# Sample attention moved from the last block's mixer into the first block's feed-forward part, the first gates of a block in two other PSUM banks, and constants set up before the row transposes

## The chip, the cores and the metric

The kernel runs on one core of one Trainium2 chip. The metric is device time in microseconds (us) of one execution. PE is the matrix engine (TensorE), PEld its weight loads, DVE the vector engine, ACT the scalar engine, POOL GpSimd, SP the engine that issues the weight transfers. PSUM has eight banks of 128 x 512 floats.

## What is computed

One layer of a hybrid decoder, for 2048 prompt rows and for 32 sample rows (8 sequences of 4 new tokens, each with a cache of 128 keys and values). Cut to what matters here:

```python
z = rmsnorm(x) @ w_in + b_in
q, k, v, xb, yb = split(z)
attn = sink_attend(q, band(k), band(v))          # prompt: window 128, in blocks of 128 queries
attn = sink_attend(q, [cache_k|k], [cache_v|v])  # sample rows: 128 cached and the new keys
xc = causal_conv(xb, prefix)
r, i = sigmoid(xc @ w_a + b_a), sigmoid(xc @ w_i + b_i)      # block-diagonal gates
lru = scan(exp(-8 r softplus(-lam)), sqrt(1 - a*a) * i * xc) # RG-LRU, in order of time
h = x + concat[attn, lru * gelu(yb)] @ w_out + b_out
y = h + (silu(gate) * up) @ w_ffn_out            # gate, up = rmsnorm(h) @ w_ffn_in
y = rmsnorm(y) * g_final
```

## The kernel before

All activations lie transposed (features on partitions). The prompt is worked through in four blocks of 512 rows; block 3, the last, is handled as "wide", that is with the 32 sample rows beside its 512, in two halves of 272 columns. The head (key, value and query projections) of block 0 is wide too and projects the 32 sample rows; their queries, keys and values lie in columns 512 to 543 from then on. Weights are split into a high and a low part, and each product is three matmuls (lines 657 to 659: high x high, high x low, low x high). The eight products of a weight tile ("unit") have 24 such matmuls per column range. Results go to three PSUM banks in rotation, `G[0..2]`; `S[0..1]`, `TB[0..1]` and `V` are the other five.

Each engine has its own queue, in an order that is written out by hand; semaphores tie them. A block is `head`, `mixers`, `ffn`. In `mixers` eight steps s = 0..7 follow on PE: `scores(s)` (L758, into S), `attend(s-2)` (L794, into V), on odd steps `spread` (L808), the unit of step s, on odd steps in its middle `gates(c)` with c = s // 2 (L817), and `probs_T(s-1)` (L776, into TB). `gates(c)` writes both S banks, so it waits for `xc_ready` (the convolution of tile c, DVE L1527 to L1529) and for `sc_read` (DVE has reduced the scores of this step, `softmax_1`, which ends in the small L1498). `scores` of an even step waits for `gates_read`, that is until ACT has read the gates (`lru_gates`, L1170 and L1171). ACT's exponentials of step s (`exps`, L1157) stand in its queue ahead of `lru_gates`, and DVE's `softmax_1(1)` stands behind `conv(0)`, whose input ACT writes (L1077) behind `exps(0)`.

The sample rows' attention and recurrence are steps within the mixer of block 3: `sample_load` (L889 ff., after step 1, transposes the cache), `sample_scores` (L906, step 4), `sample_probs` (L917, step 5), `sample_attend` (L929) and `sample_gates` (L940, both step 6), each with its part on DVE (L1650 ff., the convolution of the sample rows `sample_conv` L1709 to L1713) and ACT. Their scores, transposes and results use the S, TB and V banks too, so the prompt's steps wait for them. The cache comes in by seven transfers on POOL's queue, into the space of `hT`, at the start of block 3. POOL also loads the next block's rows, `load_x(b + 1)`, when a block's attention is done.

At the very start ACT copies the sample rows (L1336) and sums the squares of the rows (`x_stat`); DVE copies the transposed rows. The constants of the recurrence (about twenty operations on 128x4 elements that depend on each other, L1818 to L1837, one of them an exponential on ACT, L1347) are worked out after the head of block 0.

Of the kernel before, what the change touches and what calls it, by code (L numbers as in the profile page):

```python
# [31 lines left out]
ACT = mybir.ActivationFunctionType  # L32
# [59 lines left out]
def hymba_layer(nc, x_p, x_s, cache_k, cache_v, conv_in, h_in, units, vecs, w_a, w_i, sinks_p, sinks_s,  # L92
# [53 lines left out]
    with ctx:  # L146
# [38 lines left out]
        dist = place("dist", [P, 2 * WINDOW])  # L185
        dist_b = place("dist_b", [P, 2 * WINDOW])
        sinks = place("sinks", [P, NH])
# [33 lines left out]

        r = top[0]
        x_tok = place("x_tok", [P, QB, DM])
# [34 lines left out]

        SC = WINDOW + NS
        c_at = [h_at[0]]  # L260
        kc_tok = place("kc_tok", [P, DB, P], at=h_at)
        v_at = [h_at[0]]
        vc_tok = place("vc_tok", [P, DB, P], at=h_at)
        s_at = [h_at[0]]
        st_s = place("st_s", [(CONV_W - 1) * DB + DB, LC * P], at=h_at)
        k_at = [h_at[0]]
        kc_T = place("kc_T", [P, DB, P], at=h_at)
        dist_s = place("dist_s", [P, SC], at=h_at)
        s_s = place("s_s", [P, NKV, SC], at=h_at)
        q_r = place("q_r", [P, P], at=h_at)  # L270
        xc_s = place("xc_s", [P, LC, NS], at=h_at)
        hs0 = place("hs0", [P, LC, DB], at=h_at)
        assert h_at[0] <= h_end
        q_d = place("q_d", [P, DB, P], at=c_at)
        vs_tok = place("vs_tok", [NS, P], at=s_at)
        ks_out = place("ks_out", [NS, P], at=s_at)
        k_out = place("k_out", [P, P], at=s_at)
        mx_s = place("mx_s", [P, 6, NKV], at=s_at)
        pcT = place("pcT", [P, NKV, P], at=k_at)
        pnT = place("pnT", [NS, NKV, P], at=k_at)  # L280
        mixs = place("mixs", [P, KT, NS], at=k_at)
        l_s = [place(f"l_s{i}", [P, LC, NS], at=v_at) for i in range(6)]
        outc = place("outc", [P, LC, SCOLS], at=v_at)
# [253 lines left out]
        def _(pool):  # L537
# [27 lines left out]
            for b in range(NB - 1):  # L565

                amix_ready.wait(pool, b, QB)
                xT_done.wait(pool, b, KT)
                load_x(b + 1)
            b = NB - 1  # L570

            yT_done.wait(pool, b, 0)
            for dst, src in ((kc_tok[:, :, :], cache_k[0].rearrange("b s g d -> s b (g d)")),
                             (vc_tok[:, :, :], cache_v[0].rearrange("b s g d -> s b (g d)")),
                             (dist_s[:, :], dist_s_in)):
# [1397 lines left out]
```

## Time and profile before

| | |
|---|---|
| median of 3 runs | 2319.34 us (2317.89 to 2319.46) |
| the profiled execution | 2317.46 us, its span 2315.5 us |
| PE busy | 2235.7 us, 97% |
| DVE, ACT, POOL busy | 1163.2, 827.3, 32.2 us (50%, 36%, 1%) |
| mean granted clock of PE | 0.985 |

The profile's page gives busy time per engine; the trace behind it gives each instruction's start, the idle time of its engine just before it, and what ended that. In rows of the timeline merged instructions show their number as x8 and so on; one float32 matmul leaves two records. The granted clock 1.00 is 2.4 GHz and 0.50 is 1.2 GHz.

### The profile page before, as it was taken

How to read it: one execution, taken by the hardware profiler on the slowest of the kernel's cores; microseconds unless marked ns; L12 is line 12 of the kernel's file. 1: busy time of each engine (PE TensorE's matmuls, PEld its weight loads, DVE VectorE, ACT ScalarE, POOL GpSimd, SP SyncE). 2: the span in 40 equal slices, each digit the busy share in tenths (PEclk: the TensorE clock that was granted, in tenths of full speed). 3: DMA queues.
4: the chain of work that ended last, by engine and by line, in shares of the span. 5: the costliest groups of instructions: out<-in, count | busy, mean ns of one | idle time of the engine just before them, and what ended most of it. 6: DMA issues, size and time to landing. Idle time of an engine off the chain costs nothing.

```text
span 2315.5 us, 29680 instructions
## 1 busy us (share of the span) xinstructions
PE 2235.7 (97%) x12183; PEld 1886.6 (81%) x12183; DVE 1163.2 (50%) x2020; ACT 827.3 (36%) x1326; POOL 32.2 (1%) x66
## 2 busy tenths in 40 slices
PE   6999999999999999999999999999989799999997
PEld 6767888888777888888877888888878699999997
DVE  4586535446375544445466553544537545444444
ACT  4574222243274322234256322224326432222221
POOL 1000000000000000000000000000010000000000
PEclk8999999999999999999999999999999799999999
DMA  6445322222624222222533323232352132222221
GB/s 232 163 168 207 100 98 91 95 88 88 221 110 164 91 92 99 91 91 87 178 143 142 116 94 98 88 104 80 139 187 76 51 120 85 91 83 84 91 86 63
DMA packets 79014, 264.80 MB, mean 114 GB/s; under 512 B 9613, under 2 KB 13917, under 8 KB 78864
## 3 DMA queue, kind: packets, MB, share of 16 engines
q1 hardware_dynamic: 72288, 242.25, 30.4%
q0 software_dynamic: 3936, 12.03, 1.5%
q10 hardware_dynamic: 2656, 8.62, 0.9%
q8 instruction: 97, 1.59, 0.3%
q14 instruction: 37, 0.30, 0.0%
HBM read 231.04 MB, written 32.84 MB: 114 GB/s over the span
## 4 chain that ended last, share of the span: by engine, by line
PE 89%; DVE 5%; ACT 3%; issue 1%; DMA 1%; ACTq 0%; DVEq 0%
PE bank L657 27%; PE bank L659 27%; PE bank L658 27%; PE bank L817 1%; PE bank L794 1%; PE bank L758 1%; DMA out_y_p<-y_tok 1%; PE bank L776 1%; DVE s_p L1492 1%; DVE xc L1529 1%; PE bank L717 1%; PE bank L808 0%; PE bank L695 0%; PE bank L679 0%; DMA xs_tok<-in_x_sample 0%
## 5 line engine op out<-in xcount | busy, mean ns | idle before, releaser
L657 PE MATMUL bank<-x_hi,w_hi 128*128 128x512 f32 (+1 forms) x2208 | 786.6, 356 | 7.3 <-DVE x_lo L1424 4.8
L659 PE MATMUL bank<-x_hi,w_lo 128*128 128x512 f32 (+1 forms) x2208 | 777.9, 352 | 0.0
L658 PE MATMUL bank<-x_lo,w_hi 128*128 128x512 f32 (+1 forms) x2208 | 776.8, 352 | 0.0
L1052 ACT ACTIVATE w_hi<-w_raw 128x1024 fp32r<-128x1024 f32 (+1 forms) x294 | 304.6, 1037 | 1022.2 <-PE bank L659 992.5
L657 PEld LDWEIGHTS bank<-x_hi,w_hi 128*128 128x128 f32 x2208 | 416.5, 189 | 78.3 <-issue 16.2
L658 PEld LDWEIGHTS bank<-x_lo,w_hi 128*128 128x128 f32 x2208 | 416.8, 189 | 59.0 <-issue 2.9
L659 PEld LDWEIGHTS bank<-x_hi,w_lo 128*128 128x128 f32 x2208 | 416.1, 188 | 57.3
L657 PE MATMUL bank<-a_hi,w_hi 128*128 128x512 f32 (+1 forms) x1168 | 413.7, 354 | 10.3 <-DVE a_lo L1575 3.9
L1383 DVE TENSOR_TENSOR w_lo<-w_raw,w_hi 128x1024 fp32r<-128x1024 f32 (+1 forms) x294 | 351.2, 1195 | 142.5 <-ACT w_hi L1052 142.2
L659 PE MATMUL bank<-a_hi,w_lo 128*128 128x512 f32 (+1 forms) x1168 | 413.0, 354 | 0.0
L658 PE MATMUL bank<-a_lo,w_hi 128*128 128x512 f32 (+1 forms) x1168 | 412.4, 353 | 0.0
L657 PEld LDWEIGHTS bank<-a_hi,w_hi 128*128 128x128 f32 x1168 | 221.0, 189 | 45.6 <-issue 7.9
L658 PEld LDWEIGHTS bank<-a_lo,w_hi 128*128 128x128 f32 x1168 | 221.0, 189 | 30.8
L659 PEld LDWEIGHTS bank<-a_hi,w_lo 128*128 128x128 f32 x1168 | 220.9, 189 | 30.7
L1790 DVE TENSOR_TENSOR hT<-bank,hT 128x512 f32<-128x512 f32 (+1 forms) x120 | 71.0, 591 | 232.2 <-PE bank L659 232.2
L1397 DVE TENSOR_TENSOR gt<-bank,rinv 128x512 f32<-128x512 f32 (+1 forms) x110 | 64.9, 591 | 227.3 <-PE bank L659 203.0
L1397 DVE TENSOR_TENSOR a<-bank,rinv 128x512 f32<-128x512 f32 (+1 forms) x110 | 65.1, 592 | 215.9 <-PE bank L659 213.9
L1157 ACT ACTIVATE s_p<-s_p,nm 128x256 f32<-128x256 f32 x128 | 63.4, 497 | 36.1 <-DVE sd L1498 36.1
L1320 ACT ACTIVATE a_hi<-a 128x512 fp32r<-128x512 f32 (+1 forms) x88 | 56.3, 640 | 35.8 <-DVE a L1780 33.8
L1776 DVE SCALAR_TENSOR_TENSOR gt<-th,gt 128x512 f32<-128x512 f32 (+1 forms) x88 | 61.1, 695 | 6.0 <-ACT th L1317 5.9
L1780 DVE SCALAR_TENSOR_TENSOR a<-gt,a 128x512 f32<-128x512 f32 (+1 forms) x88 | 61.6, 700 | 3.0
L1784 DVE TENSOR_TENSOR a_lo<-a,a_hi 128x512 fp32r<-128x512 f32 (+1 forms) x88 | 61.0, 693 | 0.0
(282 smaller groups left out, 1627.5 us busy)
## 6 DMA issues: line engine op xcount, KB each, us to landing
w_raw<-in_units SPq DMA_DIRECT2D x222, 512.0 KB, 3.2
w_raw<-in_units SPq DMA_DIRECT2D x64, 448.0 KB, 3.1
w_hi<-keep SPq DMA_DIRECT2D x51, 512.0 KB, 3.2
w_lo<-keep SPq DMA_DIRECT2D x51, 512.0 KB, 4.2
w_kept<-keep SPq DMA_DIRECT2D x30, 512.0 KB, 4.4
keep<-w_hi SPq DMA_DIRECT2D x22, 512.0 KB, 4.9
keep<-w_lo SPq DMA_DIRECT2D x22, 512.0 KB, 5.5
x_tok<-in_x_prompt POOLq DMA_DIRECT2D x16, 512.0 KB, 5.9
```

Source lines behind the costliest of these rows:

```text
L657: nc.tensor.matmul(out, h, hi[:, kt, c0:c1], start=(first and kt == kts[0]), stop=False)
L658: nc.tensor.matmul(out, h, lo[:, kt, c0:c1], start=False, stop=False)
L659: mm = nc.tensor.matmul(out, l, hi[:, kt, c0:c1], start=False, stop=(kt == kt_of[u] - 1))
L1052: A(w_hi[:, slot(b, u), 0:n], w_raw[:, u % RAW, 0:n], ACT.Copy).then_inc(w_hi_ready, 1)
L1157: A(s_p[:, s % 2, hh, :], s_p[:, s % 2, hh, :], ACT.Exp, bias=nm[:, s % 2, hh:hh + 1], accum_out=rs[:, s % 2, hh:hh + 1])
L1320: act_hi.by(A(a_hi[:, f, 0:w], a32[:, n % 2, 0:w], ACT.Copy))
L1383: TT(w_lo[:, slot(b, u), 0:n], w_raw[:, u % RAW, 0:n], w_hi[:, slot(b, u), 0:n], ALU.subtract).then_inc(w_ready, 1)
L1397: return lambda src, c0, c1: TT(dst(c0, c1), src, rinv[:, c0:c1], ALU.mult)
L1776: link(STT(out=gt[:, 0:w], in0=th[:, 0:w], scalar=1.0, in1=gt[:, 0:w], op0=ALU.add, op1=ALU.mult))
L1780: act_f.by(STT(out=a32[:, n % 2, 0:w], in0=gt[:, 0:w], scalar=0.5, in1=a32[:, n % 2, 0:w], op0=ALU.mult, op1=ALU.mult))
L1784: act_ready.by(TT(a_lo[:, f, 0:w], a32[:, n % 2, 0:w], a_hi[:, f, 0:w], ALU.subtract))
L1790: evacuate(b, last, u, lambda src, c0, c1: TT(hT[:, m, c0:c1], src, hT[:, m, c0:c1], ALU.add))
```

## The change

1. `sample_load`, `sample_q`, `sample_scores`, `sample_max`, `sample_exps`, `sample_norm`, `sample_probs` and `sample_attend` run in block 0's feed-forward part, behind the pairs of units f = 1 to 5 of its first chunk. Their tiles lie in the space of `x_tok` (the next block's rows), the result `mixs` in the space of `dist_b`. POOL issues the seven cache transfers when block 0's attention is done, and loads the rows of block 1 only when the sample attention is finished and the new keys and values are written out. `sample_gates`, `sample_conv` and the recurrence of the sample rows stay in block 3.
2. In `sample_scores` and `sample_attend` the two key-value heads (two halves of the array's rows, or now of its columns) alternate, where one followed the other.
3. The first gates of a block (c = 0) go into `V` and a free `G` bank, and wait no more for `sc_read`. In blocks 0 to 2 they stand one product earlier within their unit.
4. The constants are set up before the row copies; ACT waits for them before its first copy.
5. The transpose of the prompt's last keys moves to the head of block 3. `dist_b` is used in block 0 alone, and its copy at the end of each block's mixer goes.

```diff
@@ gates and their banks
+        def gate_banks(c, wide):
+            return S if c else (V, G[1 if wide else 2])
...
                 def gates(c):
                     xc_ready.wait(pe, b, c + 1)
-                    sc_read.wait(pe, b, 2 * c + 2)
+                    if c:
+                        sc_read.wait(pe, b, 2 * c + 2)
                     for n in range(2):
-                        mm = nc.tensor.matmul(S[n][:, :], gates_w[:, n, c, :], xc[:, c % 2, :],
+                        mm = nc.tensor.matmul(gate_banks(c, last)[n][:, :], gates_w[:, n, c, :], xc[:, c % 2, :],
                                               start=True, stop=True)
...
-                        gemm(b, last, UH + s, x_hi, x_lo, None, list(range(KT - 2)))
+                        cut = KT - 3 if s == 1 else KT - 2
+                        gemm(b, last, UH + s, x_hi, x_lo, None, list(range(cut)))
...
-                        for step in sample_at.get(s, ()):
-                            step(b, s)
+                        if s == 6:
+                            sample_gates(s)
@@ PE, sample attention
-            def sample_load(b, s):
+            def sample_load():
+                rinvh_ready.wait(pe, 0, 1)
+                gates_read.wait(pe, 0, LC)
                 pe.wait_ge(smp_in, 16 * 7)
-                pTa_ready.wait(pe, b, s)
-                pTb_ready.wait(pe, b, s)
...
+                for bb in range(DB):
+                    for g in range(NKV):
+                        r = slice(g * HEAD, (g + 1) * HEAD)
+                        nc.tensor.matmul(S[g][:, 0:WINDOW], q_d[r, bb, :], kc_T[r, bb, :],
+                                         start=(bb == 0), stop=(bb == DB - 1))
...
-            sample_at = {1: (sample_load,), 4: (sample_scores,), 5: (sample_probs,), 6: (sample_attend, sample_gates)}
+            sample_at = {1: sample_load, 2: sample_scores, 4: sample_probs, 5: sample_attend}
...
+                        if b == 0 and ci == 0 and f in sample_at:
+                            sample_at[f]()
@@ ACT
                         act_hi.by(A(a_hi[:, f, 0:w], a32[:, n % 2, 0:w], ACT.Copy))
+                        if b == 0 and n == 2:
+                            sample_exps()
...
             split(0, 0)
+            act.wait_ge(first_in, 16 * N_FIRST)
+            act.wait_ge(setup_done, 2)
+            A(set_t[:, 1, :], set_t[:, 0, :], ACT.Exp, scale=-1.0).then_inc(setup_act, 1)
+            act.wait_ge(setup_done, 3)
             act.wait_ge(smp_pe, 1)
-            act.wait_ge(first_in, 16 * N_FIRST)
             chain.link(A(xT[:, :, T:W], V[:, 0:KT * NS].rearrange("p (k n) -> p k n", k=KT), ACT.Copy))
@@ DVE
-                        d = dist_b if qb == 0 else dist
+                        d = dist_b if b == 0 and qb == 0 else dist
...
-            sample_at = {1: sample_load, 4: sample_max, 5: sample_probs, 6: sample_attend}
-            sample_after = {2: sample_q, 7: sample_gelu}
+            sample_at = {1: (sample_load, sample_q), 2: (sample_max,), 3: (sample_norm,), 4: (sample_probs,),
+                         5: (sample_attend,)}
@@ POOL
                 amix_ready.wait(pool, b, QB)
                 xT_done.wait(pool, b, KT)
+                if b == 0:
+                    for dst, src in ((kc_tok[:, :, :], cache_k[0].rearrange("b s g d -> s b (g d)")),
...
+                    pool.wait_ge(smp_dve, SMP_DVE_L)
...
+                    pool.wait_ge(smp_dve, SMP_DVE_AT)
+                    pool.wait_ge(kv_out, 16 * 2 * DT)
                 load_x(b + 1)
```

PE at the first gates of block 0 (unit of step 1), before; `x_hi`, `x_lo` with `w_hi`, `w_lo` are the unit's products, three rows each:

```order
L657 MATMUL bank<-x_hi,w_hi 128x512
L658 MATMUL bank<-x_lo,w_hi 128x512
L659 MATMUL bank<-x_hi,w_lo 128x512
L817 MATMUL bank<-xc,gates_w 128x512 [waits sc_read,xc_ready]
L817 MATMUL bank<-xc,gates_w 128x512
L657 MATMUL bank<-x_hi,w_hi 128x512 [waits w_ready]
```

And in the changed kernel, up to the scores of step 2 (L771):

```order
L672 MATMUL bank<-x_hi,w_lo 128x512
L825 MATMUL bank<-xc,gates_w 128x512 [waits xc_ready]
L825 MATMUL bank<-xc,gates_w 128x512
L670 MATMUL bank<-x_hi,w_hi 128x512 [waits w_ready]
...
L672 MATMUL bank<-x_hi,w_lo 128x512
L787 MATMUL bank<-ident,s_p 128x128 [waits v_ready,p_ready]
L787 MATMUL bank<-ident,s_p 128x128 x7
L771 MATMUL bank<-kT,qT 128x256 [waits gates_read]
L771 MATMUL bank<-kT,qT 128x256 x3
```

The gates wait for `xc_ready` alone, and three products instead of two follow them; the scores of step 2 still wait for `gates_read`.

PE in block 3 between steps 4 and 5, before, with the sample scores (L906, L908) between the transposes of step 3 and the scores of step 5:

```order
L776 MATMUL bank<-ident,s_p 128x128 [waits pTb_ready,pTa_ready,p_ready]
L776 MATMUL bank<-ident,s_p 128x128 x7
L906 MATMUL bank<-kc_T,q_d 128x128 [waits sc_read,smp_dve]
L906 MATMUL bank<-kc_T,q_d 128x128 x7
L908 MATMUL bank<-kT,q_r 128x32
L906 MATMUL bank<-kc_T,q_d 128x128 x8
L908 MATMUL bank<-kT,q_r 128x32
L758 MATMUL bank<-kT,qT 128x256 [waits smp_dve,sc_read]
```

The same work in the changed kernel, in block 0's feed-forward part between the units of f = 2 and f = 3:

```order
L671 MATMUL bank<-x_lo,w_hi 128x512
L672 MATMUL bank<-x_hi,w_lo 128x512
L913 MATMUL bank<-kc_T,q_d 128x128 [waits smp_dve]
L913 MATMUL bank<-kc_T,q_d 128x128 x15
L917 MATMUL bank<-kT,q_r 128x32 x2
L670 MATMUL bank<-x_hi,w_hi 128x512 [waits freed,w_ready]
```

It stands between units and nothing of the attention of the prompt waits for it. `sample_load`, `sample_probs` and `sample_attend` stand likewise behind f = 1, 4 and 5.

ACT in the changed kernel, from its first weight split (L1061) to the first exponentials of block 0 (L1166):

```order
L1061 ACTIVATE w_hi<-w_raw 128x1024 [waits raw_in0]
L1346 ACTIVATE set_t<-set_t 128x4 [waits setup_done,first_in]
L1349 ACTIVATE xT<-bank 128x8x32 [waits smp_pe,setup_done]
L1100 ACTIVATE y_tok,sum_x<-x_tok 128x1024 [waits x_in,zeroed,act_chain]
...
L1061 ACTIVATE w_hi<-w_raw 128x1024 [waits kept_out2,gemm_done,raw_in0]
L88 ISA
L1166 ACT_TABLE_LOAD [waits sc_read,y_out1]
L1166 ACTIVATE s_p,rs<-s_p,nm 128x256 [waits y_out0]
```

Before, the function table for the exponentials was loaded ahead of the constants' exponential, which stood behind that last weight split; now the load stands behind the wait for `sc_read`.

## Rows read from the trace of the kernel before

**Rows 1.** Window: length, busy PE, PEld, DVE, ACT, POOL, clock, DMA share, GB/s
```profile
220.00:560.00 340.00, 340.00 (x1492) 275.52 (x1491) 159.85 (x197) 104.41 (x131) 0.00 (x0) 1.00 0.28 93
```
**Rows 2.** Timeline of block 3's mixer, PE and DVE: start, duration, [idle before <- releaser]
```profile
1722.26 3.40 PE L817 MATMUL bank<-xc,gates_w 128*128 128x512 f32 x4 [4.72 <-DVE sd L1498]
...
1730.47 1.06 PE L889 MATMUL bank<-ident,kc_tok 128*128 128x128 f32 x8 [0.93 <-DVE pT L1512]
...
1734.54 1.08 PE L794 MATMUL bank<-pT,v_tok 128*64 128x256 f32 x8 [1.25 <-DVE kc_T L1656]
...
1764.56 2.16 PE L906 MATMUL bank<-kc_T,q_d 64*128 64x128 f32 x18
...
1769.83 2.09 PE L758 MATMUL bank<-kT,qT 64*128 64x256 f32 x8 [1.40 <-DVE mx_s L1678]
...
1784.08 0.30 PE L917 MATMUL bank<-ident,s_s 128*128 128x128 f32 x1 [0.93 <-DVE pT L1512]
...
1784.64 1.14 PE L758 MATMUL bank<-kT,qT 64*128 64x256 f32 x8
...
1794.77 2.29 DVE L1713 SCALAR_TENSOR_TENSOR xc_s<-xs_b,vec,xc_s 128x32 f32<-128x32 f32 x12
...
1797.93 1.86 PE L929 MATMUL bank<-pcT,vc_tok 128*64 128x16 f32 x16 [4.04 <-DVE pT L1512]
...
1802.77 3.62 PE L940 MATMUL bank<-xc_s,gates_w 128*128 128x32 f32 x16
...
1808.11 2.08 PE L758 MATMUL bank<-kT,qT 64*128 64x256 f32 x8 [1.72 <-ACT l_s L1273]
```
**Rows 3.** Timeline, first steps of block 1's mixer, PE and ACT
```profile
637.27 1.96 PE L817 MATMUL bank<-xc,gates_w 128*128 128x512 f32 x4 [1.78 <-DVE sd L1498]
...
639.98 0.69 ACT L1171 ACTIVATE ii<-bank,lru_c 128x512 f32<-128x512 f32 x1
...
641.41 1.14 PE L758 MATMUL bank<-kT,qT 64*128 64x256 f32 x8
```
**Rows 4.** Timeline of PE in block 2, and the window of the clock behind it
```profile
1178.24 2.96 PE L817 MATMUL bank<-xc,gates_w 128*128 128x512 f32 x4 [2.60 <-DVE sd L1498]
...
1184.03 1.14 PE L758 MATMUL bank<-kT,qT 64*128 64x256 f32 x8
...
1179.00:1180.00 1.00, 1.00 (x2) 0.34 (x1) 0.00 (x0) 1.00 (x5) 0.00 (x0) 0.52 0.00 0
```
**Rows 5.** Timeline of PE, DVE and ACT at the first steps of block 0
```profile
73.24 1.28 ACT L1347 ACT_TABLE_LOAD   x1
...
74.99 0.16 DVE L1818 TENSOR_SCALAR set_t<-vec 128x4 f32<-128x4 f32 x1
...
79.16 0.16 DVE L1837 TENSOR_SCALAR lru_c<-vec 128x4 f32<-128x4 f32 x1
...
81.55 1.14 PE L758 MATMUL bank<-kT,qT 64*128 64x256 f32 x8 [2.26 <-DVE sd L1498]
...
89.89 3.46 PE L817 MATMUL bank<-xc,gates_w 128*128 128x512 f32 x4 [2.84 <-DVE sd L1498]
...
95.71 1.14 PE L758 MATMUL bank<-kT,qT 64*128 64x256 f32 x8
```
**Rows 6.** Start of the kernel: ACT's timeline, and the transfer of `vec` (us to landing last)
```profile
3.02 0.51 ACTq L1040 DMA_DIRECT2D vec<-in_vecs  x1
...
13.98 0.38 ACT L1336 ACTIVATE xT<-bank 128x256 f32<-128x256 f32 x1 [6.30 <-PE bank L994]
...
vec<-in_vecs ACTq DMA_DIRECT2D x1, 37.0 KB, 7.2
```
**Rows 7.** Timeline of PE, block 3: matmuls on alternating halves of the columns
```profile
1744.64 1.04 PE L808 MATMUL bank<-ident,rec 128*64 128x128 f32 x16
```
**Rows 8.** POOL's timeline in block 0, and the cache's transfer (us to landing last)
```profile
171.50 2.13 POOL L540 DMA_DIRECT2D x_tok<-in_x_prompt  x4 [158.94 <-DVE a_lo L1575]
...
kc_tok<-in_cache_k POOLq DMA_DIRECT2D x1, 512.0 KB, 6.9
```

More of the change, by code:

```diff
@@ L569, in _ @@
                 load_x(b + 1)
             b = NB - 1
[L572 to L575, printed above, removed]
-                pool.dma_start(dst, src).then_inc(smp_in, 16)
-            for t in range(CONV_W - 1):
-                pool.dma_start(st_s[t * DB:(t + 1) * DB, :], conv_in[0, :, t, :]).then_inc(smp_in, 16)
@@ L835, in mixers @@
                     else:
-                        gemm(b, last, UH + s, x_hi, x_lo, None, [KT - 2, KT - 1])
+                        gemm(b, last, UH + s, x_hi, x_lo, None, list(range(cut, KT)))
                     if s >= 1:
@@ L1236, in mixers @@
                         lru_hi((s - 3) // 2)
-                    if last and s == 4:
-                        sample_exps()
                     if last and s == 6:
@@ L1591, in mixers @@
                         softmax_2(s - 1)
-                    if last and s == 5:
-                        sample_norm()
                     if last and s == 6:
@@ L1604, in mixers @@
                         probs_T(s - 1)
-                    if last and s in sample_at:
-                        sample_at[s]()
                     if s >= 3 and s % 2 == 1:
@@ L1610, in mixers @@
                         gelu_arg(c)
[L1611 to L1612 removed]
+                    if last and s == NUN - 1:
+                        sample_gelu()
                 softmax_2(NUN - 1)
@@ L1784, in ffn @@
                         act_ready.by(TT(a_lo[:, f, 0:w], a32[:, n % 2, 0:w], a_hi[:, f, 0:w], ALU.subtract))
+                        if b == 0 and ci == 0:
+                            for step in sample_at.get(f, ()):
+                                step()
                         if ci == len(FCH) - 1 and not last:
@@ L1837, in _ @@
             TS(lru_c[:, 1, :], vec[:, VBI:VBI + LC], 0.5, None, ALU.mult).then_inc(setup_done, 1)
+            for kt in range(KT):
+                xT_done.wait(dve, 0, kt + 1)
+                xT_moved.by(nc.vector.tensor_copy(xT[:, kt, 0:T], xbank[kt % 4][:, :]))
+            reciprocals(0, True, std_x, rstd_x, stdx_ready, rstdx_ready)
+            x_normed(0, True, 0)
+            for kt in range(KT):
+                if kt + 1 < KT:
+                    x_normed(0, True, kt + 1)
+                x_rest(0, True, kt)
+            for u in range(1, RING):
+                split(0, u)
+            dve.wait_ge(zeroed, 7)
+            head(0, True)
             dve.wait_ge(const_in, 16 * N_CONST)
```

154 lines of the change are left out of this document (65 added, 89 removed).

## The prediction

> **What bounds the kernel now.** I read the busy times by window first. In block 0's feed-forward part PE is busy 340.00 of 340 us and DVE 159.85 [rows 1]; the other feed-forward parts and heads look alike. There only work added to PE or taken from it counts. Then I read PE's idle times in the timeline: they lie in the mixers, most in block 3, where in front of nearly each sample step, or of the prompt's step behind it, PE stands: 4.72, 0.93, 1.25, 1.40, 0.93, 4.04 and 1.72 us [rows 2]. Blocks 1 and 2 have one such wait each, in front of the first gates, 1.78 and 2.60 us [rows 3, 4], and block 0 has two of 2.26 and 2.84 [rows 5]. Last, the clock. After the wait of 1.78 us the four gate records took 1.96 us, after 2.60 us they took 2.96, and the window behind shows 0.52, half of full clock; after 2.84 and 4.72 they took 3.46 and 3.40 [rows 2 to 5]. So idle stretches of 2.6 us and more were each followed by a stretch at 1.2 GHz, that of 1.8 was not. What such a stretch costs I take from a pair: from the gates to the scores of step 2 it is 4.1 us in block 1 (637.27 to 641.41) and 5.8 in blocks 0 and 2 (89.89 to 95.71, 1178.24 to 1184.03), so 1.7 us a time.
>
> **The start, +0.8 us.** ACT now waits for the constants before its first copy. `vec` was issued at 3.02 and took 7.2, so it is there at 10.2 [rows 6]. The chain of constants ran from 74.99 to 79.32, 4.3 us with its trip to ACT [rows 5]; with 0.1 for the query bias ahead of it, it ends at 14.6, and the copy that began at 13.98 begins at about 14.8. All of the start hangs on the squares behind that copy, so 0.8 us goes through. Were `vec` there only when that copy ran (it waits for it too), it would be 4.4; were it there by 9.5, nothing. A gain is excluded, since nothing ahead of that copy gets shorter.
>
> **Block 0's first steps, -5.4 us.** Without the constants DVE starts `softmax_1(0)` at 75.0, not 79.3. It took 2.2 us (79.32 to 81.55, when PE's scores start [rows 5]), so it ends at 77.2. ACT's table load, 1.28 us, was hidden at 73.24 and now stands behind the wait for it, so the exponentials start at 78.5 where they started at 81.5: 3.0 earlier, and with them `xb`, `conv(0)` and `softmax_1(1)`, which ended at 89.9 and will end at 86.9. PE's 2.26 goes. The gates need only `conv(0)`, 2.2 before that, at 84.7, when PE arrives too; clock and 2.84 us are saved. But the scores of step 2 wait for ACT's reading of the gates, and this stands behind `exps(1)`, behind `softmax_1(1)`. That is **what is late next**. In block 1 it is 640.67 - 637.27 = 3.4 us from the end of `softmax_1(1)` (where the old gates started) to the end of ACT L1171 [rows 3]. So the scores start at 86.9 + 3.4 = 90.3, not 95.7.
>
> **Blocks 1 and 2, -0.7 and -2.4 us.** The same limit: PE could start the gates 2.2 us earlier and does the third product behind them, but the scores of step 2 start at 640.7 instead of 641.4 and at 1178.24 + 3.4 = 1181.65 instead of 1184.03. Of 1.78 us only 0.7 comes home; in block 2 the clock's 1.7 comes with it, as its idle of 2.6 is cut into pieces of about 1.
>
> **Block 3, -21.5 us.** By pieces:
> - Step 1 to the scores of step 2. PE went idle at 1722.26 - 4.72 = 1717.5. `conv(0)` is done 2.2 before the old gates, at 1720.05. From the gates to 1729.54 (1730.47 - 0.93) it was 7.3 us with the slow clock; without it 5.6 to 5.8. That gives 1725.8; ACT's limit 1722.26 + 3.4 = 1725.7 agrees. The old scores started at about 1732.2 (1734.54 less 1.25 and the scores' 1.1). Saved: 6.4. An idle of 2.5 is just under the 2.6 that cost the clock, so the lower end is 4.7.
> - `attend(0)` waited 1.25 for the sample copies: gone.
> - Step 4: sample scores, wait and slow clock. From 1764.56 to the scores of step 5 at 1769.83 it is 5.3; these took 2.09 where others take 1.14, and the attention behind them was slowed too by some 0.4. Saved: 6.6.
> - Step 5: 0.93 and the transposes to 1784.64: 1.5.
> - Step 6. PE was idle from 1793.9 and reached the scores of step 7 at 1808.11: 14.2 us. The sample attention (1797.93 to 1802.77, 4.8 us) goes, the gates (3.62 to the wait of 1.72) stay. And a wait stays: they need `sample_conv`, which ends at 1797.06, that is 12.4 us after the scores of step 6 (1784.64); DVE's two sample copies in there go, so 12.1. PE needs 1793.9 - 1784.64 = 9.2, so it stands about 3.0 us, the clock falls as before, and 3.0 + 3.6 + 1.7 = 8.3. Saved: 5.9.
> - The transpose of the last keys stays, in the head: +0.1.
> Behind step 7 nothing changes; the waits there are of the recurrence.
>
> **Block 0's feed-forward part, +6.3 us.** PE has no idle time there, so all the moved matmuls are paid. Load: 1730.47 to 1732.2, less the one transpose, 1.6. Probabilities: 0.6. Scores: 34 records, 3.7 us before (1764.56 to 1769.83 less the wait). Attention: 36 records, 4.8 us at half clock, so 2.4 at full. In the changed order neighbours use different halves of the array. The nearest row with alternating halves (of columns) is `spread`: 16 records in 1.04 us, 0.061 each [rows 7], where the scores, one half after the other, took 0.11. At that pace scores and attention are 2.1 each. Ends: 3.7 and 4.8 if alternation brings nothing and the clock falls; together 5 to 10.7. The Trainium skill speaks to both sides of this: "TensorEngine Tiling (Array Packing)", Key Properties, says that different tiles load weights and multiply in parallel, and that a change of tiling mode drains the engine. By its first sentence scores and attention would be 1.9 and 1.2, 1 us under my sum; its second speaks against cutting in such steps between full-size products, but the same changes of mode stood in block 3 and are only moved. No row here has halves of rows alternating.
>
> DVE is the cover to be watched: the copies and `sample_q` add some 4 to 5 us behind f = 1 (an estimate: eight times the 0.6 us for 128x512 elements, the L1713 row's 2.29 being 12 small ones), where a pair of units lasts 11 us and DVE's own work 5.2 (159.85 / 340 x 11). They fit, with two units of slack in G. Each PE step waits for a DVE step that stands a whole pair of units ahead of it. If the cover failed, each step would cost a wait of 1 to 3 us. The cache transfers start where the rows of block 1 were loaded, at 171.5; that load now waits until f = 5, some 200 us ahead of its use.
>
> **Sum.** 0.8 - 5.4 - 0.7 - 2.4 - 21.5 + 6.3 = -22.9. The profiled execution took 2317.46 us: 2294.6. The median of the runs is 1.9 above it: **2296.5 us**. The removed copies of `dist_b` lie in DVE's idle time behind the recurrence: nothing.
>
> **The rivals.**
> - The clock stays up in step 6 of block 3, because its idle is 3.0 instead of 4.0. Gates of 1.8 instead of 3.6 and about 2.6 saved in step 7: 2292. Against it: 2.60 and 2.84 were enough to lose it. 13%.
> - The small matmuls in block 0 gain nothing by alternating (+4.3) and the clock falls behind scores and attention (+3.3): 2304. For it: the scores of step 5 were slow (2.09) after only 1.40 us of idle, right behind the sample scores. 13%.
> - With the sample steps gone, the prompt's own chains (two table loads and three exponential steps on ACT, scan and mix on DVE) bind steps 4 and 6 of block 3, 2 to 3 us each: 2302. For it: my margins there are 1 to 2 us; against it: blocks 1 and 2 have no such wait with shorter steps. 9%.
> - The change does not do what it says: the early gates bring nothing, since the scores of step 2 wait for ACT whatever bank is used, and a late ACT (its table load) eats the constants' gain. Then blocks 0 to 2 give 3 us, not 8.5: 2302. 8%.
> - Slower: the cache is not there. `sample_load` stands in PE's queue ahead of every later unit, so a late transfer stops all. It is issued at about 172 and took 6.9 elsewhere [rows 8]; PE asks for it at about 230. It decides from 253 on (22.9 us of stall), a landing of 80 us. At 260 it would be 2303, at 280 slower: 2324. 2%.
> The forecast itself: 55%.
>
> **How the numbers follow.** 2296.5 is the forecast's. The range 2289 to 2304 takes in the first four rivals and the ends of the start and of the small matmuls, and leaves out the sums of two misfortunes. A measurement can tell 0.2% (4.6 us) from no change; all cases but the last give over three times that: faster 0.96, same 0.02, slower 0.02.
>
> **What would show it.** ACT's first copy at 14.8. The first gates with under 1 us of idle in blocks 0 to 2, and a new wait of about 1 us of the scores of step 2 for ACT's gate reading. Feed-forward of block 0 longer by 6 us with no idle on PE. Block 3 with waits left at the first gates (2.5), the sample gates (3.0) and step 7 (1.7). It would be wrong if PE waited in block 0's f = 1 to 5, if the clock there left 1.00, or if steps 2 to 5 of block 3 showed new waits.

## The result and the profile after

| | before | changed |
|---|---|---|
| median of 4 runs each | 2318.61 us (2317.11 to 2319.46) | 2292.38 us (2290.60 to 2293.07) |
| the profiled execution, its span | 2317.46, 2315.5 us | 2292.82, 2291.0 us |
| mean granted clock of PE | 0.985 | 0.989 |

The ratio is 0.9886 (95%: 0.9869 to 0.9904): 26.2 us faster. The forecast was 2296.5, with a range of 2289 to 2304.

The first lines of the page of the changed kernel:

```profile
span 2291.0 us, 29666 instructions
## 1 busy us (share of the span) xinstructions
PE 2226.1 (97%) x12183; PEld 1880.5 (82%) x12183; DVE 1162.1 (51%) x2017; ACT 826.0 (36%) x1326; POOL 32.2 (1%) x66
```

PE's busy time fell by 9.6 us (from 2235.7), and that at 97% of the span in both. The rest of the gain was idle time. So the page's first table says little; the program has to be cut into stretches. I cut at three kinds of matmul whose starts both traces show: the transposes of the values (L702, now L715) at the end of a head, the row sums behind a mixer (`ssum`) and those behind a feed-forward part (`ssum_y`).

| stretch | before | changed | measured | forecast |
|---|---|---|---|---|
| start to the values of block 0 | 71.50 | 74.39 | +2.9 | +0.8 |
| mixer, block 0 | 145.14 | 139.79 | -5.4 | -5.4 |
| feed-forward, block 0 | 379.37 | 385.36 | +6.0 | +6.3 |
| mixer, block 1 | 134.16 | 133.45 | -0.7 | -0.7 |
| mixer, block 2 | 136.62 | 133.37 | -3.3 | -2.4 |
| mixer, block 3 | 187.15 | 161.51 | -25.6 | -21.5 |
| feed-forward of block 3 and tail | 422.99 | 424.52 | +1.5 | 0 |

The heads of blocks 1 to 3 and the feed-forward parts of blocks 1 and 2 agree within 0.02 us. The sum is -24.5, the difference of the spans. The rows behind the table, of the changed kernel:

Timeline of PE in block 0 and block 2 (start, duration, idle before and what ended it), which answers to [rows 4, 5]:

```profile
82.11 1.14 PE L771 MATMUL bank<-kT,qT 64*128 64x256 f32 x8
87.56 1.98 PE L825 MATMUL bank<-xc,gates_w 128*128 128x512 f32 x4 [0.64 <-DVE xc L1548]
93.22 1.14 PE L771 MATMUL bank<-kT,qT 64*128 64x256 f32 x8 [0.72 <-ACT ii L1181]
...
1177.93 1.98 PE L825 MATMUL bank<-xc,gates_w 128*128 128x512 f32 x4 [0.16 <-DVE xc L1548]
```

The waits of 2.26, 2.84 and 2.60 us are gone, and with them the slow gate records (1.98 instead of 3.46 and 2.96). The wait named as late next stands where it was forecast: the scores of step 2 wait 0.72 us for ACT's reading of the gates.

The window of block 0's feed-forward part, and the moved matmuls in PE's timeline [rows 1, 7]:

```profile
220.00:560.00 340.00, 340.00 (x1556) 275.56 (x1555) 164.27 (x236) 104.06 (x134) 6.07 (x12) 1.00 0.29 97
```
```profile
244.99 0.39 PE L671 MATMUL bank<-x_lo,w_hi 128*128 128x512 f32 x1
245.22 0.40 PE L672 MATMUL bank<-x_hi,w_lo 128*128 128x512 f32 x1
245.55 2.06 PE L913 MATMUL bank<-kc_T,q_d 64*128 64x128 f32 x32
247.44 0.31 PE L917 MATMUL bank<-kT,q_r 64*128 64x32 f32 x4
247.68 0.50 PE L670 MATMUL bank<-x_hi,w_hi 128*128 128x512 f32 x1
248.02 0.40 PE L671 MATMUL bank<-x_lo,w_hi 128*128 128x512 f32 x1
...
281.73 1.11 PE L934 MATMUL bank<-pcT,vc_tok 128*64 128x16 f32 x32
282.77 0.43 PE L938 MATMUL bank<-pnT,vs_tok 32*64 32x128 f32 x4
283.14 0.50 PE L670 MATMUL bank<-x_hi,w_hi 128*128 128x512 f32 x1
```

PE has no idle time and a clock of 1.00: DVE's added work of 4.4 us (164.27 against 159.85) fits beside it. The scores took 2.13 us to the next product (245.55 to 247.68), the attention 1.41 (281.73 to 283.14).

Block 3, timeline of PE [rows 2]:

```profile
1717.69 1.99 PE L825 MATMUL bank<-xc,gates_w 128*128 128x512 f32 x4 [0.43 <-DVE xs_b L1554]
1723.50 1.14 PE L771 MATMUL bank<-kT,qT 64*128 64x256 f32 x8
...
1753.69 1.14 PE L771 MATMUL bank<-kT,qT 64*128 64x256 f32 x8
...
1765.47 1.14 PE L771 MATMUL bank<-kT,qT 64*128 64x256 f32 x8
...
1777.83 3.62 PE L947 MATMUL bank<-xc_s,gates_w 128*128 128x32 f32 x16 [3.09 <-DVE xc_s L1717]
1783.17 2.08 PE L771 MATMUL bank<-kT,qT 64*128 64x256 f32 x8 [1.72 <-ACT l_s L1281]
...
1786.94 1.26 PE L815 MATMUL bank<-ident,rec 128*64 128x128 f32 x16
```

Steps 2 to 5 have no wait left. Step 6 is as forecast within 0.1: 3.09, 3.62, 1.72 (3.0, 3.6 and 1.7). The surprise is the first row: 0.43 us of idle where 2.5 were expected.

### The profile page after: what moved, and what is told of

Same layout as the page of the kernel before. It is cut to its first block, busy times and chain, and to the rows that moved or that the text cites. A ratio compares the mean times of both kernels' runs of the same rounds, so it can differ in the third digit from the quotient of the medians.

```text
span 2291.0 us, 29666 instructions
## 1 busy us (share of the span) xinstructions
PE 2226.1 (97%) x12183; PEld 1880.5 (82%) x12183; DVE 1162.1 (51%) x2017; ACT 826.0 (36%) x1326; POOL 32.2 (1%) x66
## 4 chain that ended last, share of the span: by engine, by line
PE 89%; DVE 5%; ACT 3%; issue 1%; DMA 1%; ACTq 0%; DVEq 0%
PE bank L670 28%; PE bank L672 28%; PE bank L671 28%; PE bank L803 1%; PE bank L771 1%; PE bank L825 1%; PE bank L787 1%; DMA out_y_p<-y_tok 1%; PE bank L732 1%; DVE xc L1548 1%; ACT s_p L1166 1%; DVE s_p L1511 1%; PE bank L815 1%; PE bank L708 0%; PE bank L692 0%
## 5 line engine op out<-in xcount | busy, mean ns | idle before, releaser
L1061 ACT ACTIVATE w_hi<-w_raw 128x1024 fp32r<-128x1024 f32 (+1 forms) x294 | 304.7, 1037 | 1024.4 <-PE bank L672 996.4
L670 PEld LDWEIGHTS bank<-x_hi,w_hi 128*128 128x128 f32 x2208 | 416.5, 189 | 77.4 <-issue 15.5
L1166 ACT ACTIVATE s_p<-s_p,nm 128x256 f32<-128x256 f32 x128 | 63.4, 498 | 22.1 <-DVE sd L1517 22.1
```

The lines of the kernel that those rows point to most:

```text
L670: nc.tensor.matmul(out, h, hi[:, kt, c0:c1], start=(first and kt == kts[0]), stop=False)
L1061: A(w_hi[:, slot(b, u), 0:n], w_raw[:, u % RAW, 0:n], ACT.Copy).then_inc(w_hi_ready, 1)
L1166: A(s_p[:, s % 2, hh, :], s_p[:, s % 2, hh, :], ACT.Exp, bias=nm[:, s % 2, hh:hh + 1], accum_out=rs[:, s % 2, hh:hh + 1])
```

## Experiments

All are timed in five rounds against the kernel before unless said otherwise (its medians: 2318.7, 2319.3 and 2318.4 in the three sets), and profiled. Line numbers shift by a few between them.

**1. Constants back behind the head.**

```diff
             split(0, 0)
+            act.wait_ge(smp_pe, 1)
             act.wait_ge(first_in, 16 * N_FIRST)
-            act.wait_ge(setup_done, 2)
-            A(set_t[:, 1, :], set_t[:, 0, :], ACT.Exp, scale=-1.0).then_inc(setup_act, 1)
-            act.wait_ge(setup_done, 3)
-            act.wait_ge(smp_pe, 1)
...
+            act.wait_ge(setup_done, 1)
             head(0, True)
+            act.wait_ge(setup_done, 2)
+            A(set_t[:, 1, :], set_t[:, 0, :], ACT.Exp, scale=-1.0).then_inc(setup_act, 1)
+            act.wait_ge(setup_done, 3)
```

This is ACT's part; DVE's operations on the constants move in the same way, from ahead of the row copies to behind `head(0, True)`.

> The constants go back behind the head of block 0; all else is as in the changed kernel. Theory: this part moved 2.9 us into the start (ACT's copy of the sample rows at 15.79 instead of 13.98, the full clock back about 1.1 us later) and takes about 3.0 us from DVE ahead of the scores of block 0, so it is worth nothing here: the time stays within 1 us of the changed kernel's 2292.4, the copy begins at 14.0, the transpose of the values (L715's counterpart) at 71.5, and from there to the end of block 0's mixer it is about 3 us longer. Rival: the constants alone gave block 0's 5.4 us, the early gates none of them (the scores of step 2 wait for ACT whatever bank is used): then 5.4 - 2.9 = 2.5 us slower than the changed kernel, 2295.

2292.52 us (2290.14 to 2293.86). The start took 71.96 us and block 0's mixer 143.11: 3.3 longer than in the changed kernel. The rival would have had 5.4; the early gates by themselves keep 2.0 of block 0's gain. The time fits the theory, but it comes from another set of runs than the changed kernel's, and two such sets differ by more than what is asked here (run 11), so only the stretches speak.

**2. ACT waits for the finished constants only ahead of the head.**

```diff
             A(set_t[:, 1, :], set_t[:, 0, :], ACT.Exp, scale=-1.0).then_inc(setup_act, 1)
-            act.wait_ge(setup_done, 3)
             act.wait_ge(smp_pe, 1)
...
+            act.wait_ge(setup_done, 3)
             head(0, True)
```

> ACT's wait for the end of the constants stands no longer ahead of its copy of the sample rows but behind the weight splits, ahead of the head of block 0 (its exponential of the constants stays where it is). Theory: the start lost 2.9 us because that wait held the copy, and the clock's return came late with it; now ACT waits at most until its exponential's input is there and the start loses about 0.5, the mixer of block 0 stays at 139.8: about 2290.0, 2.4 us under the changed kernel. Rival A: the exponential itself needs the transferred constants and holds ACT nearly as long (they landed at about 11, the exponential is 3 operations behind): the copy begins at 14.5 or later and 1.5 us come home. Rival B: the full clock's return at about 43 instead of 39 does not hang on ACT's copy: then 1.8 at most comes home, 2290.6, and the clock is still at one half at 40 us.

2291.33 us (2290.26 to 2291.98). The values of block 0 are transposed at 70.73 instead of 74.39, and the mixer of block 0 keeps its 139.76. Timeline of ACT at the start, first of the changed kernel:

```profile
11.81 0.21 ACT L1346 ACTIVATE set_t<-set_t 128x4 f32<-128x4 f32 x1 [3.99 <-DVE set_t L1810]
15.79 0.38 ACT L1349 ACTIVATE xT<-bank 128x256 f32<-128x256 f32 x1 [3.77 <-DVE lru_c L1828]
```

and of this run:

```profile
10.95 0.20 ACT L1346 ACTIVATE set_t<-set_t 128x4 f32<-128x4 f32 x1 [3.18 <-DVE set_t L1810]
14.29 0.39 ACT L1348 ACTIVATE xT<-bank 128x256 f32<-128x256 f32 x1 [3.13 <-PE bank L1003]
```

PE's transpose ends ACT's wait again, as before the change [rows 6]; rival A just falls (14.29, not 14.5 or later). Rival B falls too: PE's granted clock is 0.88 in the window from 38 to 39 us and 1.00 from 39 on, where the changed kernel had 0.50 until 43. The time is 1.3 over the forecast of 2290.0. By this pair of profiles 3.7 us came home (2.0 went again in block 3's mixer, 162.11, and its feed-forward part, 405.57 against 404.12); how much of it is chance, run 11 says.

**3. The first gates in the score banks again.**

```diff
-            return S if c else (V, G[1 if wide else 2])
+            return S
...
-                    if c:
-                        sc_read.wait(pe, b, 2 * c + 2)
+                    sc_read.wait(pe, b, 2 * c + 2)
...
-                        cut = KT - 3 if s == 1 else KT - 2
+                        cut = KT - 2
```

> The first gates of a block go into the two score banks again, wait for the scores' reduction, and stand one product later; all else is as in the changed kernel. Theory: block 1 is 0.7 us longer, block 2 3.3 (its wait of 2.6 costs the clock), block 0 and block 3 2 to 3 each (idle of about 2.3 and 2.5 in front of the gates, with the clock lost if it reaches 2.6): 2300, range 2298 to 2303. Rival: the early gates bring nothing because the scores of step 2 wait for ACT's reading of them in either form, and the gain of blocks 1 and 2 is a matter of the clock's chance: then 2293.

2297.57 us (2296.31 to 2298.32), under the range. The mixers are longer by 2.4, 0.75, 0.9 and 4.6 us. Block 2 is the miss. Timeline of PE:

```profile
88.37 3.65 PE L824 MATMUL bank<-xc,gates_w 128*128 128x512 f32 x4 [2.20 <-DVE sd L1516]
...
1182.03 1.96 PE L824 MATMUL bank<-xc,gates_w 128*128 128x512 f32 x4 [1.84 <-DVE sd L1516]
...
1722.61 2.92 PE L824 MATMUL bank<-xc,gates_w 128*128 128x512 f32 x4 [2.73 <-DVE sd L1516]
```

The old gates stand in block 2 again, but wait 1.84 us, not 2.60, and the clock stays up. Something that the change did elsewhere shortened that wait. In block 3 the wait of 2.73 cost the clock (0.50 in the window from 1724 to 1725). In block 0 already one of 2.20 us did: the gate records took 3.65 us and the clock was 0.50 from 89 to 91. Why block 3 loses twice as much by it as block 0 was not taken apart.

**4. Heads one after the other in the sample attention.** In both loops:

```diff
-                for bb in range(DB):
-                    for g in range(NKV):
+                for g in range(NKV):
+                    for bb in range(DB):
```

> In the sample rows' scores and their attention the two key-value heads follow one another again, where the changed kernel alternates them; the steps stay in block 0's feed-forward part. Theory: alternating heads is why 32 + 4 records of the scores take 2.06 + 0.31 us (the trace of before has them in about 3.7), and why the attention takes 1.11 + 0.43: without it the scores take 3.5 to 3.7, the attention about 2.2 to 2.4, together 2.5 us more, 2294.9. Rival: the alternation does nothing, both were slow in block 3 because of the clock and the waits around them: then the same durations as in the changed kernel and 2292.4.

2292.45 us (2290.12 to 2294.13): no difference in the times, where 2.5 us were expected. The stretch shows one: block 0's feed-forward part is 387.52 us, 2.16 longer. Timeline of PE:

```profile
242.89 3.16 PE L913 MATMUL bank<-kc_T,q_d 64*128 64x128 f32 x29
...
246.46 0.50 PE L670 MATMUL bank<-x_hi,w_hi 128*128 128x512 f32 x1
...
280.52 1.83 PE L934 MATMUL bank<-pcT,vc_tok 128*64 128x16 f32 x32
...
282.64 0.50 PE L670 MATMUL bank<-x_hi,w_hi 128*128 128x512 f32 x1
```

Scores 3.57 us (242.89 to 246.46) against 2.13, attention 2.12 against 1.41: 1.44 + 0.71 = 2.15, the whole difference. The alternation is what did it. The rest of this profile happened to have a short start and tail (71.58, 18.79), which hides 2 us in a time; the rule for reading is in run 11.

**5. Two cache transfers once more beside block 3's start.** They are the two large ones of the seven, 512 KB each; the other five have 16 to 80 KB. Nothing reads them.

```diff
+            yT_done.wait(pool, b, 0)
+            for dst, src in ((again_k[:, :, :], cache_k[0].rearrange("b s g d -> s b (g d)")),
+                             (again_v[:, :, :], cache_v[0].rearrange("b s g d -> s b (g d)"))):
+                pool.dma_start(dst, src).then_inc(smp_in, 16)
+            pool.wait_ge(smp_in, 16 * 9)
```

> The changed kernel with two of the cache transfers (512 KB each) issued once more at the start of block 3, into free space, where the kernel before had all seven. Nothing reads them. Theory: block 3 gained 4.1 us more than was forecast because, without these transfers beside it, the output transfer for which ACT waits ahead of its exponentials lands 4.8 instead of 6.7 us after it is asked for. With them, ACT's wait grows from 4.04 to about 6 us, the first gates of block 3 stand about 2.3 us idle instead of 0.43, and block 3's mixer is 1.5 to 2 us longer (3.5 if the clock falls too): 2294.3, up to 2296. Rival: the transfer was late for another reason (its place in the queue), and the two transfers change nothing: 2292.4, ACT's wait stays at 4.0.

2292.53 us (2290.40 to 2294.68). Timelines of ACT and PE, of this run:

```profile
1709.70 1.28 ACT L1173 ACT_TABLE_LOAD   x1 [5.53 <-DMA out_y_p<-y_tok]
...
1717.40 1.98 PE L832 MATMUL bank<-xc,gates_w 128*128 128x512 f32 x4 [1.91 <-DVE xs_b L1561]
```

ACT of the changed kernel at the same place, and of the kernel before:

```profile
1709.99 1.28 ACT L1166 ACT_TABLE_LOAD   x1 [4.04 <-DMA out_y_p<-y_tok]
```
```profile
1712.31 1.28 ACT L1157 ACT_TABLE_LOAD   x1 [5.97 <-DMA out_y_p<-y_tok]
```

This is the theory's chain: transfers beside it, the output lands 1.5 us later, ACT's exponentials start that much later, the gates' wait goes from 0.43 to 1.91. From the transposes of the values to the scores of step 2 it took 20.0 us, where the five other profiles whose block 3 is that of the changed kernel (its two and runs 1, 2 and 4) have 18.5 to 18.8. Block 3's mixer was 163.77 us, 2.3 more, against 160.4 to 162.1 in those five; what goes beyond 1.5 lies behind step 6, in when the clock came back. At the first gates it stayed up. In the times, forecast at 2294.3, this is not seen.

**6. The sample rows' gates behind the last unit.** The start of the sample rows' recurrence leaves step 6 as well:

```diff
 (PE)
-                    if last and s == 7:
-                        pe.wait_ge(smp_act, 2)
...
-                    if last:
-                        if s == 6:
-                            sample_gates(s)
+                    if last and s == NUN - 1:
+                        gates_read.wait(pe, b, LC)
+                        sample_gates(s)
 (ACT)
-                    if last and s == 6:
-                        sample_gates()
-                        sample_decay()
...
                 gelu_tanh(LC - 1)
+                if last:
+                    sample_gates()
+                    sample_decay()
                 attn_recs(QB - 1)
 (DVE)
-                    if last and s == 6:
+                    if last and s == 7:
                         sample_conv()
-                    if last and s == 7:
-                        sample_square()
...
                 attn_lo(QB - 1)
+                if last:
+                    sample_square()
```

> A further step, from the changed kernel: the sample rows' convolution goes behind step 7 of block 3 on DVE, their gates behind the last unit of the mixer on PE, ACT's part of them behind the last gelu, and the square of the decay behind the last attention. Theory: the two waits in step 6, 3.09 and 1.72 us, go, and with the first of them the loss of clock behind it (gates 3.62 us instead of about 1.8, the scores of step 7 likewise): 6 to 8 us less in block 3's mixer, less 0.8 for a later start of the gates: 2285.5. Rival: the wait is only moved, since the recurrence of block 3 behind step 7 is what the end of the mixer waits for, and DVE's sample work there stands in its way: 2290 or above, with longer waits in the tail of the mixer (now 2.06, 1.95, 1.71, 1.41 and 1.02).

2286.42 us (2285.81 to 2287.29), near the forecast of 2285.5. Block 3's mixer took 156.96 us, 4.6 less than in the changed kernel's first profile and 3.5 less than in its second. Timeline of PE:

```profile
1773.44 1.14 PE L769 MATMUL bank<-kT,qT 64*128 64x256 f32 x8
...
1786.47 1.94 PE L945 MATMUL bank<-xc_s,gates_w 128*128 128x32 f32 x16 [1.18 <-issue]
...
1801.31 0.57 PE L670 MATMUL bank<-a_hi,w_hi 128*128 128x272 f32 x1 [4.63 <-DVE a_lo L1592]
...
1807.87 0.36 PE L670 MATMUL bank<-a_hi,w_hi 128*128 128x272 f32 x1 [1.10 <-DVE a_lo L1587]
```

Both waits of step 6 are gone: the scores of step 7 follow those of step 6 (1764.24) by 9.2 us, not 17.7 (16.4 to 17.7 in the five profiles named under run 5). Of these 8.5 us, 4 were given back: a wait of 1.18 and records of 1.94 at the new place of the gates, and waits of 4.63 and 1.10 in front of the output units, where there were 2.06, 1.95 and 1.71. So theory and rival each hold for about half.

**7. Both further steps (2 and 6).**

> Both further steps at once: ACT's wait for the constants behind the weight splits, and the sample rows' gates behind the last unit of block 3's mixer. Theory: the two lie at opposite ends of the program and share no wait, so they add: about 2.4 and 6.9 us, 2283.1. Rival: one of the two gives nothing (see its own run), and this kernel is as the other alone.

2284.26 us (2282.53 to 2285.63), ratio 0.9843 to the kernel before (95%: 0.9827 to 0.9859). It is the fastest version here, 2.2 us under run 6, timed on the same chip in the same set, and 1.2 over the forecast. They add: start 70.48, block 3's mixer 156.46.

**8. Only the sample rows' move.** The edits of 1 and 3 together; point 5 of the change stays in too.

> Only the sample rows' attention is moved (and its heads alternate); the constants are behind the head of block 0 and the first gates in the score banks, as before. Theory: blocks 0, 1 and 2 are as in the kernel before, with +6.0 for the feed-forward part of block 0; block 3 keeps its gain of 25.6 but for 2 to 3 us at its first gates: 2318.6 + 6.0 - 23 = 2301.6, range 2300 to 2304. With the runs that undo the constants and the gates alone, this says whether the parts add: the constants are worth nothing by themselves, so it should equal the run with late gates within 1 us. Rival: the parts meet in block 0 (constants early and gates early each bring something only with the other): then this kernel is less slow than both parts' losses together, or more, by over 1.5 us.

2300.50 us (2299.40 to 2301.01), in the range, but 2.9 over run 3, where the theory that the constants are worth nothing by themselves allowed 1; the two are of different sets. Block 3's mixer 166.07 (-21.1 against before), block 0's mixer 145.15, as before. In block 0 the parts add: constants early save 3.0 (142.18, run 3), gates early 2.0 (143.11, run 1), both 5.4, so the rival (they need each other) falls. Block 2 has 134.56, 2.1 less than before, with neither gates nor constants changed.

**9. From 7, ACT's decay behind the last attention.**

```diff
                     sample_gates()
-                    sample_decay()
                 attn_recs(QB - 1)
                 attn_hi(QB - 1)
                 if last:
+                    sample_decay()
```

> From the run with both further steps: ACT does the sample rows' decay (8 small activations, 2.5 us in the trace) behind the copies of the last prompt attention instead of ahead of them. In that run PE stood 4.64 us in front of the output unit that needs those copies, and behind it 1.79 us for the last tile of the recurrence. Theory: what bounds there is the recurrence (ACT's square root behind its table load, then DVE's scan, the mix and its low part), which this edit doesn't touch. The 4.64 shrinks to about 2.1 and the wait behind it grows by as much, to 3.5 or more, and the time stays within 0.7 us of 2284.3. Rival: the wait that the trace names is the one that counts, and 2.5 us come home: 2281.8.

2284.42 us (2283.67 to 2287.61), as run 7; block 3's mixer 158.50, 2.0 more. Timeline of PE, of this run:

```profile
1797.35 0.36 PE L670 MATMUL bank<-a_hi,w_hi 128*128 128x272 f32 x1 [1.95 <-DVE a_lo L1592]
1806.35 0.57 PE L670 MATMUL bank<-a_hi,w_hi 128*128 128x272 f32 x1 [5.75 <-DVE a_lo L1587]
```

and of run 7:

```profile
1798.74 0.36 PE L670 MATMUL bank<-a_hi,w_hi 128*128 128x272 f32 x1 [4.64 <-DVE a_lo L1592]
1805.30 0.37 PE L670 MATMUL bank<-a_hi,w_hi 128*128 128x272 f32 x1 [1.79 <-DVE a_lo L1587]
```

The large named wait shrank by 2.7 us, and the next grew by 4.0, to 5.75 where 3.5 or more were forecast. What bounds there is the chain that the second wait is for; an edit that only makes PE arrive there earlier bought nothing.

**10. The kernel before once more** (one round).

> The kernel before, profiled once more, to see which of its waits are of every execution. Theory: the wait in front of the first gates follows from when the output transfer lands, ACT's wait for it less about 2.3 us in blocks 1 and 2. That transfer lands late in block 3 always (the seven cache transfers beside it: ACT waits 5.5 to 6.5, the gates 4 to 5), but in block 2 its 4.93 was chance: here about 4.1, the gates' wait 1.8 and no loss of clock, block 2's mixer 134.3 instead of 136.6. Rival: block 2's 2.60 and its clock loss are of the kernel and stand here again.

2321.51 us (2318.14 to 2325.44) against 2318.42 for the other runs of the same kernel, ratio 1.0012 (0.9999 to 1.0024). The theory on block 2 fell. Timelines of ACT and PE:

```profile
1168.47 1.28 ACT L1157 ACT_TABLE_LOAD   x1 [4.84 <-DMA out_y_p<-y_tok]
1712.36 1.28 ACT L1157 ACT_TABLE_LOAD   x1 [6.19 <-DMA out_y_p<-y_tok]
```
```profile
1178.05 3.04 PE L817 MATMUL bank<-xc,gates_w 128*128 128x512 f32 x4 [2.52 <-DVE sd L1498]
```

Block 2 repeats (136.54 us in all), and the clock falls behind a wait of 2.52 us. The link that the theory names holds: in the eight rows of blocks 1 and 2 with the old gates (both traces of this kernel, runs 3 and 8) PE's wait is ACT's less 2.31 to 2.33 us. In the two traces of the kernel before, ACT waits 4.93 and 4.84 us for this output transfer; in the eleven traces with the sample rows moved, 4.02 to 4.36. So the wait is of the kernel; why the transfer lands about 0.7 us later there is open, for it is issued 0.21 us behind the start of the values' transposes in both kernels.

**11. The changed kernel once more.**

> The changed kernel, timed and profiled once more beside the others of this call. Theory: the long start of its first profile (values transposed at 74.39) was in part chance: the profiles of other kernels with the same start have 71.6 to 73.1 with a copy at 14.7 to 15.4; here it is again in 71.5 to 74.4, with the copy at 14.7 to 15.8. Blocks 0 to 3 repeat within 0.5 us (139.8, 133.4, 133.4, 161.5). Time 2292.4 within 1. Rival: 74.4 is the start of this kernel and repeats within 0.5.

2289.17 us (2288.61 to 2290.13), 3.2 under the first measurement: two sets of the same kernel can differ by that much. Start 72.88, copy at 15.17; mixers 139.68, 133.48, 133.35, 160.43; tail 20.36. The stretches from block 0 to block 2 repeat within 0.2 us, block 3 within 1.1, and the start and tail do not. Over all profiles the values of block 0 are transposed at 71.6 to 74.4 (mean of six: 72.9) where ACT waits for the finished constants, at 70.4 to 72.0 (mean of four: 71.3) where they come behind the head, and at 70.5 to 70.7 (three) where ACT waits late. The tail behind the last feed-forward part takes 18.7 to 20.5 whatever the kernel (18.86 and 20.37 in the two profiles of the kernel before). So effects under 3 us are read from stretches here, not from times, and the start only from several profiles.

## Why the prediction was right, point by point

**The whole.** 2292.38 lies in the range, 4.1 under the forecast; the second measurement (2289.17) just in it. That the sum came so near has some luck in it: block 3 and block 2 gave 4.1 and 0.9 us more than forecast, while start and tail took 2.1 and 1.5 more, in good part by the scatter of single profiles. Between the profiled executions the forecast was short by only 1.7; the other 2.3 us are that the profiled execution lay 1.9 under its median before and 0.4 above it after. None of the rivals came: the clock fell in step 6 with 3.09 us of idle (0.50 in the window from 1778 to 1779), the small matmuls gained by alternating, steps 2 to 5 of block 3 have no wait, the early gates bring time in every block, and the cache was in place.

**The start (+0.8): mis-sized.** The step said that `vec` is there at 10.2 and the chain ends 4.4 us later. The chain took 4.7 (11.05 to 15.75), which is near, but it began at 11.05, so the copy stood at 15.79, not 14.8. In five more profiles with this wait the copy is at 14.69 to 15.36: the landing varies, and a wait put behind it takes over that variation. The second half was not in the sum at all. The clock at the first products came back later than the copy's delay explains. Windows of PE, first before, then changed (clock is the third number from the end):

```profile
39.00:40.00 1.00, 1.00 (x10) 1.00 (x10) 0.80 (x4) 0.26 (x1) 0.00 (x0) 1.00 0.67 160
```
```profile
42.00:43.00 1.00, 1.00 (x7) 1.00 (x6) 0.00 (x0) 0.00 (x0) 0.00 (x0) 0.50 0.97 328
43.00:44.00 1.00, 1.00 (x9) 1.00 (x9) 0.00 (x0) 0.00 (x0) 0.00 (x0) 0.91 1.03 418
```

Four microseconds later, with a copy 1.8 us later. In run 11 it was back in the window from 40 to 41. By the means of run 11, of profiles that scatter by 1.5 to 2.8 us, the wait cost 1.6 us (72.9 - 71.3), twice the term; moving it costs the mixer nothing (run 2). Against block 0's 3.3 the early constants are worth 1.7; the times of run 1 and of the changed kernel cannot tell that, and that of run 8 against run 3, 2.9 us, points the same way but is of two sets.

**Block 0's mixer (-5.4): right, and by its mechanism.** Runs 1 and 3 show both shares. ACT's limit on the scores of step 2 is the 0.72 us in the first rows above.

**Blocks 1 and 2 (-0.7 and -2.4).** Block 1 is right. In block 2 the number was near (-3.3) and the reason half wrong. The step gave it all to the early gates and the clock they keep. Run 3, with the old gates, loses only 0.9. The other 2.3 came with the output transfer landing 0.5 to 0.9 us earlier, which kept the gates' wait at 1.84 and the clock up. The releaser in front of PE's wait is DVE, in front of that is ACT, and in front of ACT a DMA; I had followed the chain one link only.

**Block 3 (-21.5): the mechanism right, the size short by 4.1.** From the values' transpose to the scores of step 2 it took 18.5 us (1704.97 to 1723.50), 8.3 less than the 26.8 before, not 6.4. The step kept `conv(0)` where it was; but ACT's wait for the output transfer, ahead of the exponentials and of `xb`, was 4.04 instead of 5.97. Run 5 puts 1.5 us of it back with the two large ones of the seven transfers. So the transfers had cost time where no row of PE names them. Two more rows of the kernel before bear on the 4.1, neither of them in my list:

```profile
1749.62 1.95 PE L817 MATMUL bank<-xc,gates_w 128*128 128x512 f32 x4 [0.72 <-DVE sd L1498]
...
1811.88 1.92 PE L808 MATMUL bank<-ident,rec 128*64 128x128 f32 x16
```

and of the same kernel in run 10:

```profile
1813.10 1.32 PE L808 MATMUL bank<-ident,rec 128*64 128x128 f32 x16
```

The second gate wait of 0.72 us went too. Step 6 came out within 0.1. Behind it `spread` took 1.26 us instead of 1.92, and from the scores of step 7 to the attention behind the last unit it was 14.7 us (1783.17 to 1797.90) where it had been 15.5 (1808.11 to 1823.58). But this 0.7 us is not of the change: in run 10 the kernel before has 1.32 us for `spread` and 14.8 for the stretch. 1.9 + 0.7 + 0.7 leaves 0.8 of the 4.1 in smaller pieces. The first piece is known no better than that either, for in run 10 the kernel before took 28.4 us where it had taken 26.8. One bound of this step was wrong: it said that an idle of 2.5 us is just under what costs the clock, but 2.52 us in run 10 and 2.20 in run 3 cost it too. It was not put to the test here, since the wait was 0.43.

**Block 0's feed-forward part (+6.3): +6.0.** Scores came out at 2.13 for 2.1, attention at 1.41 for 2.1. Run 4 shows that it is the alternation that counts, and what it is worth at full clock, 2.15 us. The rival "gain nothing by alternating" was priced at 4.3, since it took the attention's 4.8 us as they stood at half clock.

The Trainium skill, "TensorEngine Tiling (Array Packing)", Key Properties, says that different tiles load weights and multiply in parallel. The estimate drawn from that, 1.2 us for the attention and 1.9 for the scores, was the nearer one for the attention (1.41) and not for the scores (2.13). The same list says that a change of tiling mode drains the engine. The rows agree with a cost there, and it is small: the first small matmul starts 0.33 us behind the last product where products follow by 0.23, and the second product behind the scores starts 0.34 behind the first. That is 0.1 at each end, 0.2 per insertion.

**The tail (0): +1.5,** not of the change: the feed-forward part of block 3 is the same (404.13 and 404.12), and the rest took 18.86 and 20.37 us in the two profiles of the kernel before, 20.40 and 20.36 in those of the changed one.

## What to carry to other kernels

Follow a wait back until it ends in a DMA or in the engine's own work, not just to its first releaser; here a 512 KB output transfer, which no row of PE names, set the start of the first gates in blocks 1 to 3, and two large transfers put back beside it cost 1.5 us in block 3, which a list of PE's waits does not show. A wait put behind a start-up transfer belongs as late in the queue as its first real use: moving this one behind the weight splits kept block 0's mixer at 139.76. And a moved step should be priced at both ends: of about 8 us saved in step 6 by run 6, 4 came back behind step 7, and in run 9 a largest wait shrunk by 2.7 us gained nothing, since the next one grew by 4.0.

## What the runs showed that was not expected

The clock's return at the start of the program varies between kernels with the same first instructions by more than the edits explain (38 to 43 us; in the two profiles of the changed kernel, in the windows from 40 to 41 and from 43 to 44). The small matmuls cost 0.1 us at each change of array shape at full clock. A wait of 2.20 us was enough to lose the clock (run 3, block 0), where waits of 1.91 us and less in front of the same gates were not. And the output transfer in block 2 lands later in the kernel before in both of its profiles, although it is issued at the same point of the program; what delays it was not tried.
